# Order of the three split-operand passes over two token halves in a decoder layer's products

## What is computed

```
x <- LN1(alpha*x + 0.5*SwiGLU_a(x))        d_ff = 2816
x <- LN2(alpha*x + Mix(x))                 one input projection, short conv + sparse attention, one output projection
x <- LN3(alpha*x + 0.5*SwiGLU_b(x))

def swiglu(x, w_gate, w_up, w_down):
    return (jax.nn.silu(x @ w_gate) * (x @ w_up)) @ w_down
```

## Time and profile before

| | |
|---|---|
| three runs | 1608.97, 1609.25, 1612.55 us; median 1609.25 |
| profiled execution | 1610.04 us, of which 1608.3 us is the span of the trace |
| busy: PE, PEld | 1447.8 us (90%), 1353.6 us (84%) |
| busy: DVE, ACT, POOL | 521.5 us (32%), 410.7 us (26%), 117.4 us (7%) |
| mean granted clock of TensorE | 0.972 |
| line 603 on the chain that ended last | 61% |

### The profile page before, as it was taken

One profiled execution on the slowest core, in us unless ns is written; L12 is line 12 of the kernel. 1 busy time (PEld: TensorE's weight loads), 2 busy tenths in 40 slices (PEclk: granted clock), 3 DMA queues, 4 the chain that ended last, 5 costly groups with the idle time before them and its releaser, 6 DMA issues.

```text
span 1608.3 us, 32780 instructions
## 1 busy us (share of the span) xinstructions
PE 1447.8 (90%) x13241; PEld 1353.6 (84%) x13241; DVE 521.5 (32%) x746; ACT 410.7 (26%) x635; POOL 117.4 (7%) x151
## 2 busy tenths in 40 slices
PE   1599999999999998899888879876989999999996
PEld 0599899999999998899856556555879999999995
DVE  0000033333233334522334434435453333233334
ACT  0000022221122212422214434431252222122214
POOL 0000000000000000308050202200030000000000
PEclk9999999999999999999979999997999999999998
DMA  8837513233223331233393526522122233233311
GB/s 216 276 124 240 175 29 91 83 96 93 81 78 91 99 101 35 61 84 92 75 313 117 173 80 218 173 62 79 53 66 84 86 108 87 66 91 91 103 54 56
DMA packets 250514, 176.14 MB, mean 110 GB/s; under 512 B 21635, under 2 KB 246642, under 8 KB 249812
## 3 DMA queue, kind: packets, MB, share of 16 engines
q1 hardware_dynamic: 228948, 150.10, 32.4%
q10 hardware_dynamic: 18432, 16.79, 3.2%
q0 software_dynamic: 3072, 8.39, 1.6%
HBM read 171.29 MB, written 8.10 MB: 112 GB/s over the span
## 4 chain that ended last, share of the span: by engine, by line
PE 85%; ACT 4%; DVE 3%; DMA 3%; issue 2%; ACTq 1%; SPq 0%; DVEq 0%
PE ps L603 61%; PE ps L633 9%; PE ps L901 2%; PE ps L886 2%; PE ps L932 2%; PE ps L691 2%; DMA pe_sb<-in_cmp_pe_dram 2%; DMA w1p<-in_cmp_w_dram 1%; ACT kt L1214 1%; ACTq L335 1%; PE ps L969 1%; ACT x L1096 1%; PE ps L948 1%; PE ps L702 1%; PE ps L911 1%
## 5 line engine op out<-in xcount | busy, mean ns | idle before, releaser
L603 PE MATMUL ps<-xh,ghi 128*128 128x272 f32 x1904 | 399.6, 291 | 22.0 <-DVE xl L1422 13.4
L603 PE MATMUL ps<-xh,glo 128*128 128x272 f32 x1904 | 397.2, 290 | 0.0
L603 PE MATMUL ps<-xl,ghi 128*128 128x272 f32 x1904 | 395.7, 290 | 0.0
L603 PEld LDWEIGHTS ps<-xh,ghi 128*128 128x128 f32 x1904 | 302.6, 190 | 26.5 <-issue 21.0
L603 PEld LDWEIGHTS ps<-xl,ghi 128*128 128x128 f32 x1904 | 302.6, 191 | 0.0
L603 PEld LDWEIGHTS ps<-xh,glo 128*128 128x128 f32 x1904 | 300.4, 191 | 0.0
L1278 DVE TENSOR_TENSOR glo<-graw,ghi 128x1024 fp32r<-128x1024 f32 x119 | 147.5, 1242 | 267.8 <-ACT ghi L1035 266.8
L633 PE MATMUL ps<-span 64*64 64x128 f32 (+1 forms) x2560 | 148.9, 415 | 0.0
L633 PEld LDWEIGHTS ps<-span 64*64 64x64 f32 x2560 | 142.0, 156 | 5.5
L603 PE MATMUL ps<-hh,dhi 128*128 128x272 f32 x704 | 145.4, 287 | 0.0
L603 PE MATMUL ps<-hl,dhi 128*128 128x272 f32 x704 | 145.3, 287 | 0.0
(11 more groups left out here) (296 smaller groups left out, 1210.8 us busy)
## 6 DMA issues: line engine op xcount, KB each, us to landing
page<-in_cache_sel_kv_dram SPq DMA_DIRECT2D x192, 128.0 KB, 3.0
span<-in_cache_cmp_kv_dram ACTq DMA_DIRECT2D x128, 128.0 KB, 3.9
span<-in_cache_cmp_kv_dram SPq DMA_DIRECT2D x128, 128.0 KB, 3.9
graw<-in_ffa_gate_dram SPq DMA_DIRECT2D x22, 512.0 KB, 3.8
graw<-in_ffa_up_dram SPq DMA_DIRECT2D x22, 512.0 KB, 3.8
draw<-in_ffa_down_dram SPq DMA_DIRECT2D x16, 704.0 KB, 4.6
graw<-in_w_in_dram SPq DMA_DIRECT2D x44, 256.0 KB, 3.2
graw<-in_ffb_gate_dram SPq DMA_DIRECT2D x22, 512.0 KB, 3.8
```

Source lines behind the costliest of these rows:

```text
L603: last = nc.tensor.matmul(out[:, h, 0:HALF], a[:, k, :], b[:, k, h * HALF:(h + 1) * HALF], start=(k == 0 and a is hi and b is xhi), stop=( ...
```

## The change

The two inner loops of `product` trade places: the loop over the halves is now outside the loop over the passes.

```diff
@@ -598,8 +598,8 @@
                         pe.wait_ge(norm_lo, parts + k + 1)
                     if last_h is not None and k == chunks - 1:
                         pe.wait_ge(hl_ready, last_h)
-                    for a, b in ((hi, xhi), (hi, xlo), (lo, xhi)):
-                        for h in range(2):
+                    for h in range(2):
+                        for a, b in ((hi, xhi), (hi, xlo), (lo, xhi)):
                             last = nc.tensor.matmul(
                                 out[:, h, 0:HALF], a[:, k, :], b[:, k, h * HALF:(h + 1) * HALF],
                                 start=(k == 0 and a is hi and b is xhi),
```

## The result

The kernel with the change takes 1615.78 us (median of 8 runs, 1614.26 to 1617.02), the kernel before in the same comparison 1610.75 us (8 runs, 1608.97 to 1612.55). The ratio is 1.0031 with a 95% interval of 1.0021 to 1.0042: slower by 0.3%, 5.0 us. The forecast of no change is wrong, and 1615.78 lies 0.8 us above the range.

The account below looks back on a forecast made before the run. The prediction took TensorE's own matmul pace at line 603, 0.125 us each, as the bound. Waits 0, weights 0 (within 2.6 us) and banks 0 summed to 0, giving 1609.5 us, range 1604 to 1615 us.

Parts of the forecast that it names:

- Waits, 0: Line 603's chunks: all waits stay ahead of the first matmul and readers still wait for the last; cost 0.
- Weights that change more often, 0: Line 603: 2608 more changes of the stationary tile, taken as 0 from equal medians, within 2.6 us either way.
- Banks, 0: Line 603: 5216 matmuls now follow one into the same PSUM bank; taken as 0 from the layer norm's fp32 matmuls.
- -62 and +23 us: Ends of the PSUM bank term: 5216 matmuls saving 0.0118 us each, or paying 0.0044 us each.
- The 0.0118 us: Part of each line 603 matmul's 0.1251 us at full clock beyond 0.1133 us of column streaming; left unexplained.
- The 0.0094 us: Unexplained time per line 603 matmul if the Trainium skill's estimate of 0.116 us for 272 columns is used.
- the 49 us: Lower end of the PSUM bank term by the skill page's figure, 5216 x 0.0094, instead of 62.
- Weights: Prediction paragraph on line 603's stationary tile, changing four times per chunk instead of twice, and the moving tile likewise; 0.
- 2608 x 1 ns: Bound of 2.6 us either way for line 603's additional stationary-tile changes, from medians agreeing within 1 ns.
- A one-pass matmul is held up by the previous one in its bank: Slower rival at line 603: 5216 matmuls staying in a PSUM bank pay 0.0044 us each, 1632 us; chance 0.05.
- The faster rival: Leaving a PSUM bank costs time at full clock, so line 603 gains up to 62 us, 1547 us; chance 0.07.
- the one on weights: Slower rival at line 603: weights that stay are cheaper; 2608 x 0.0118 = 31 us added, 1640 us; chance 0.02.

Follow-up runs that it names:

- A0 B0 C0 C1 B1 A1: Changed kernel with half 1's three passes run backwards, three weight-tile changes per chunk; 1613.48 us beside 1611.12 for the kernel before.
- A C B: Changed kernel with each half's passes ordered hi with xhi, lo with xhi, hi with xlo; 1617.97 us beside 1610.73 for the kernel before.

## Why the prediction was wrong

**Waits, 0: right.** They are those of before within 0.4 us, and the order on the other engines cost nothing.

**Weights that change more often, 0: right.** Orders with three, four and five changes of the weight tile per chunk (A0 B0 C0 C1 B1 A1, the change, A C B) all run at 126.10 to 126.12 ns, and the change with xl shifted by 128 or 384 bytes runs at 125.00 with four.

**Banks, 0: right.** Swapping the banks between the two orders left 126.11 and 125.27 ns where they were. Both ends, -62 and +23 us, rested on a price that is not there. The 0.0118 us from which the -62 came is, but for 3 ns at most, no price per matmul but the rate of the stream. (The 0.0094 us beside it is 0.0118 - 0.0025 = 0.0093; the 49 us stay.)

**The step that failed** is the last sentence under *Weights*: "The moving tile likewise changes four times instead of twice, at the same steps of 0.25 us: 0, inside the same bound." It should have been the main term: the runs put 4.9 us there, 5712 x 0.86 ns. How often the moving tile changes is not what counts: it changes four times at 125.00 ns as well. What counts is where xl (or hl), streamed behind and ahead of xh (hh), lies relative to it in SBUF, modulo 256 bytes:

| order | steps in a chunk | gate/up pace, ns |
|---|---|---|
| before | to another place | 125.26 |
| the change | 4 of 6 to the same place | 126.12 |
| the change, xl shifted by 256 or 512 | 4 of 6 to the same place | 126.12 |
| the change, xl shifted by 128 or 384 | to another place | 125.00 |

Moving hl alone gave the down halves the same loss, 125.17 to 126.08 ns.

Two things let it through. The rows named for it cannot show it: durations are medians within 1 ns and steps are given to 0.01 us, while 0.6 ns per matmul was the effect that the prediction itself had called visible in the time. And I let a bound of 2608 x 1 ns, made for changes of the weight tile, stand for all 7824 matmuls; with 1 ns on each it would have been 7.8 us, and the range would have held the result. Nor was there a row to size it from: the order before never streams two stretches at the same place one behind the other inside a chunk. It could only be bounded, not taken as equal.

**The rivals.** "A one-pass matmul is held up by the previous one in its bank" had the right sign, and its mechanism is excluded. The faster rival is excluded by the same runs, the one on weights by those named above. What I had written would show the forecast wrong, a step at line 603 that moves by over 0.6 ns on the mean, is what happened.

**What stays open.** The same order on the same places ran at 125.00 and 125.83 ns (order before, xl moved), at 125.08 and 125.83 (down halves of the order before, gate/up weights moved), at 125.55 and 125.00 (the change, xl moved). What chooses between such paces was not found. The loss itself does not waver: in the eight kernels that stream half by half with xl at xh's place modulo 256, every gate/up stretch of every trace, wherever PE does not wait, has 126.08 to 126.14 ns. At another place the pace is lower in all that were measured, but it is not one number: 125.00 in most, 125.55 in one stretch, up to 125.83 in the order before. Shown is thus that the place is the cause of the loss; by what mechanism, and why the steps of single matmuls do not follow the places, stays open. No version beat both kernels: the repaired change is level with before.

## What to carry to other kernels

Where one stream of matmuls is the bound, divide the effect that a measurement can tell by the number of matmuls, and bound every altered neighbourhood (weights, bank, moving stretch) for all of them at that resolution; the pace is read from two starts a thousand matmuls apart, not from medians. When matmuls are put into another order, write down the SBUF place of each moving tile beside that of the one streamed before it: here tiles that met at the same place modulo 256 bytes cost 0.3% of the kernel, and 128 bytes of padding took it back. The same padding made the order before no faster, so measure it for the order in question.

## What the hardware showed that I had not expected

- The pace of a stream at full clock depends on where its operands lie: 126.12 ns for 272 columns when one stretch follows another at the same place modulo 256 bytes, 125.00 ns when xl lies 128 further (125.17 in the down halves, where hl does).
- The `F32R` stream does not double its rate from half to full clock: 0.833 ns per column at half clock, 0.461 at full. The Trainium skill, "TensorE: Matmul & The Clock Gate", section "Back-to-back issue gap", has columns / 2.4 GHz + 2.5 ns for what it calls the isolated gap of a single matmul, an estimate of 0.116 us for 272 columns; this case's traces have 0.1250 to 0.1261 us. Its estimate for 304 columns is 0.129 us, and 0.1403 was measured, so the difference grows with the columns.
- Paces came in few values (125.00, about 125.27, 125.55, 125.83, 126.11 ns), some 0.28 ns apart, and the same program took different ones in different stretches of one execution.
